# Scale half of the conditioning first, four gate tiles multiplied before the shift is known

## What is computed

```python
mod = c @ w_ada + b_ada                      # c: 1 prompt row and 8 sample rows; w_ada (2048, 6144)
shift, scale, gate = jnp.split(mod, 3, axis=-1)
h = _rms(x, g_norm) * (1 + scale[:, None, :]) + shift[:, None, :]
z = h @ w_in      # parts q, k, v, qi, ki, wi, ga, u, gb, ma, mb
...               # indexer top-k, gathered attention, pooling mixer: attn, pool
a  = (attn * jax.nn.silu(ga)) @ w_a_proj
bb = (pool * jax.nn.silu(gb)) @ w_b_proj
m = jax.nn.sigmoid(ma) * a + jax.nn.sigmoid(mb) * bb
y = x + gate[:, None, :] * (m @ w_out)       # then a final RMSNorm
```

## Time and profile before

| | |
|---|---|
| median of three timed executions | 1974.14 us |
| profiled execution: device time / span | 1972.96 / 1971.1 us |
| busy in the span: PE / DVE / ACT / POOL | 1907.3 / 983.0 / 535.1 / 906.5 us |
| DMA | 257.91 MB, mean 131 GB/s |
| granted clock, mean of the span | 0.985 |

### The profile page before, as it was taken

How to read it: one execution, slowest core, us unless ns; L and a number is a source line. 1 busy time by engine, 2 the same in 40 slices (tenths; PEclk the granted TensorE clock), 3 DMA queues, 4 the chain that set the end, 5 groups by cost and what they waited for, 6 DMA issues and landing times.

```text
span 1971.1 us, 34676 instructions
## 1 busy us (share of the span) xinstructions
PE 1907.3 (97%) x14418; PEld 1767.4 (90%) x14418; DVE 983.0 (50%) x1485; ACT 535.1 (27%) x730; POOL 906.5 (46%) x760
## 2 busy tenths in 40 slices
PE   5789999999999999999999999999999999999997
PEld 2369998989999999999999999999999999887775
DVE  4168885677787778753346444445011411142223
ACT  4122333434333333332211222212222311122223
POOL 0234555545554545444444444445566443344442
PEclk9789999999999999999999999999999999999999
DMA  9963334543233232324332333335475565544333
GB/s 351 360 209 88 105 106 127 151 145 81 79 86 96 75 96 69 96 81 127 87 87 66 96 88 80 88 96 139 139 233 174 175 211 152 174 144 136 107 106 129
DMA packets 325028, 257.91 MB, mean 131 GB/s; under 512 B 8603, under 2 KB 275031, under 8 KB 323623
## 3 DMA queue, kind: packets, MB, share of 16 engines
q1 hardware_dynamic: 311759, 227.03, 39.2%
q0 software_dynamic: 5120, 16.77, 2.6%
q10 hardware_dynamic: 8064, 12.87, 2.2%
HBM read 245.63 MB, written 11.48 MB: 130 GB/s over the span
## 4 chain that ended last, share of the span: by engine, by line
PE 90%; DMA 3%; DVE 2%; SPq 2%; ACT 1%; POOL 1%; issue 1%; DVEq 0%; ACTq 0%
PE acc L1487 68%; PE ps L1941 9%; DMA ring<-in_w_ada 2%; PE ps L1725 1%; PE ps L1601 1%; PE ps L1741 1%; PE ps L1713 1%; PE acc L1500 1%; PE ps L1487 1%; PE acc L1932 1%; PE ps L1871 1%; SPq L334 1%; PE ps L1788 1%; POOL wlo L481 1%; DMA kib<-in_cache_kidx,pgr 1%; PE ps L1647 1%
## 5 line engine op out<-in xcount | busy, mean ns | idle before, releaser
L481 POOL TENSOR_TENSOR wlo<-raw,whi 128x512 fp32r<-128x512 f32 (+1 forms) x612 | 785.4, 1314 | 842.8 <-ACT whi L607 842.8
L1487 PE MATMUL acc<-act_hi,whi 128*128 128x260 f32 (+1 forms) x3520 | 751.2, 289 | 1.7 <-DVE stok L1117 0.9
L1487 PE MATMUL acc<-act_hi,wlo 128*128 128x260 f32 (+1 forms) x3520 | 740.3, 287 | 0.0
L1487 PE MATMUL acc<-act_lo,whi 128*128 128x260 f32 (+1 forms) x3520 | 739.2, 286 | 0.0
L1487 PEld LDWEIGHTS acc<-act_hi,whi 128*128 128x128 f32 x3520 | 551.7, 189 | 18.5 <-issue 13.6
L1487 PEld LDWEIGHTS acc<-act_lo,whi 128*128 128x128 f32 x3520 | 549.9, 188 | 0.7
L1487 PEld LDWEIGHTS acc<-act_hi,wlo 128*128 128x128 f32 x3520 | 549.9, 188 | 0.0
L607 ACT CAST whi<-raw 128x2048 fp32r<-128x2048 f32 (+1 forms) x153 | 279.3, 1825 | 964.4 <-PE acc L1487 764.4
L1941 PE MATMUL ps<-whi,act_hi 128*128 128x512 f32 x256 | 102.1, 399 | 0.0
L1941 PE MATMUL ps<-whi,act_lo 128*128 128x512 f32 x256 | 101.1, 395 | 0.0
L1941 PE MATMUL ps<-wlo,act_hi 128*128 128x512 f32 x256 | 101.0, 394 | 0.0
(11 more groups left out here) (310 smaller groups left out, 2099.1 us busy)
## 6 DMA issues: line engine op xcount, KB each, us to landing
raw<-in_w_in SPq DMA_DIRECT2D x105, 1024.0 KB, 5.9
ring<-in_w_ada SPq DMA_DIRECT2D x32, 1024.0 KB, 9.4
raw<-in_w_a_proj SPq DMA_DIRECT2D x16, 1024.0 KB, 7.9
gate_unit<-in_w_ada SPq DMA_DIRECT2D x16, 1024.0 KB, 7.0
raw<-in_w_out SPq DMA_DIRECT2D x16, 1024.0 KB, 5.1
raw<-in_w_b_proj SPq DMA_DIRECT2D x16, 512.0 KB, 4.6
x_tok<-in_x_prompt SPq DMA_DIRECT2D x4, 1024.0 KB, 16.4
att_dram<-silu_ga ACTq DMA_DIRECT2D x16, 256.0 KB, 2.6
```

The source lines that it names most:

```text
L481: return nc.gpsimd.tensor_tensor(wlo[p][:, a:b], raw[p][:, a:b], whi[p][:, a:b].bitcast(F32), ALU.subtract)
L1487: last = mm(o, w, x[:, k, s], start=(k == 0 and n == 0), stop=(k == kt - 1 and n == 2))
```

## The change

The scale chunks come first, then the shift chunks. With the scale alone VectorE makes `H` without the shift (`scale`), and it and ScalarE split this. TensorE multiplies it by the first four `mb` tiles (`EARLY`): two in quarters between the units 4 to 19, the third with units 20 to 23 and the fourth with units 24 to 29 inside. ScalarE writes the four results to DRAM (`early_out`). Then the shift is added (`shift`), and the split is made again. The index key and the first index query, which were made in parts between the units, are made whole behind the last unit.

The shift's share of those four tiles (shift @ `w_in`, nine columns) is made in the pooled stage: SP loads the four tiles' weights again in four 1 MB units, TensorE makes four `corr_product` and one `corr_columns`, and the four results come back from DRAM to `big2`; ScalarE takes their tanh with the prompt's column as the bias. The pooled stage then has 12 pairs, and four `w_b` tiles without an `mb` tile. The 16 late rounds are spread over 12 pairs: two in each of the pairs 1 to 4.

SP now loads the sample rows and the four token tiles first, then units 0 to 3 (in the places of `whi` and `wlo`) and two `mb` tiles; units from 4 on go round the four buffers in the tokens' place. The first DMAs of ScalarE's queue (conditioning rows and identity) have a semaphore of their own, and the rest of the tables is waited for later.

```diff
-ADA_CHUNKS = [4, 0, 5, 1, 6, 2, 7, 3]
+ADA_CHUNKS = [4, 5, 6, 7, 0, 1, 2, 3]
...
-LATE, LATE_RING = 10, 4
...
+LATE, LATE_RING = 4, 4
...
+RING_AT = [u + 2 if u < LATE else RING + (u - LATE) % LATE_RING for u in range(ADA_UNITS)]
...
+EARLY = 4
+Q_A, Q_B, Q_C, Q_D, Q_E, Q_E1, Q_F1, Q_F2, Q_G, Q_END = 2, 11, 15, 31, 39, 51, 53, 61, 69, 77
+
+N_A, N_B, N_C, N_D, N_E, N_E1, N_F1, N_F2, N_G = 2, 11, 13, 29, 37, 49, 51, 59, 67
...
+    def early_at(e):
+
+        return ((e + 1) // 2, 1 - e % 2)
...
+        def load_early(e, first=False):
+            load(*early_at(e), cols(w_in, C_MB + P * e), first=first)
+
+        sp.dma_start(xs[:], t["x_sample"].rearrange("b s d -> (b s) d")).then_inc(S("xs_landed"), 16)
+        for i in range(4):
+            sp.dma_start(x_tok[:, i, :], t["x_prompt"][0, i * P:(i + 1) * P, :]).then_inc(S(f"x_landed{i}"), 16)
+        sp.dma_start(pgi[:], t["page_table"].rearrange("(o b) n -> o b n", o=1).broadcast_to([P, NB, PAGES])
+                     ).then_inc(S("pages_landed"), 16)
         for u in range(ADA_UNITS):
             if u == LATE:
+                load_early(0, first=True)
+                load_early(1, first=True)
                 sp.wait_ge(S("xT_done"), 4)
...
+            if u == 14:
+                load_early(2)
+            if u == 18:
+                load_early(3)
+            if u == 28:
+                load(Q_A, 1, cols(w_in, C_KI))
...
+        load(Q_A + 1, 0, cols(w_in, C_QI))
+        sp.wait_ge(S("ring_done"), ADA_UNITS)
+        sp.dma_start(cosT[:], t["k_cos"]).then_inc(S("consts_landed"), 16)
+        sp.dma_start(sinT[:], t["k_sin"]).then_inc(S("consts_landed"), 16)
         load(Q_A + 1, 1, cols(w_in, C_QI + P))
...
+
+        for j in range(1, KT - EARLY):
+            load(Q_E + j, 0, cols(w_in, C_MB + P * (EARLY + j)))
+            load(Q_E + j, 1, cols(w_b, P * (EARLY + j)))
+            if j <= 4:
+                if j == 1:
+                    sp.wait_ge(S("early_step"), 1)
+                else:
+                    sp.wait_ge(S("corr_mm"), j - 1)
+                sp.dma_start(corr_unit[:].rearrange("p (k n) -> p k n", n=512), quarter(w_in, j - 1, C_MB)
+                             ).then_inc(S("weights_landed"), 16)
+            if j == 5:
+                sp.wait_ge(S("mix_mm"), 8)
+                sp.wait_ge(S("u_tok_ready"), 8)
+                sp.wait_ge(S("early_stored"), 16 * EARLY)
+                sp.dma_start(big2[:, 0:EARLY, :], early_dram.rearrange("e p n -> p e n")
+                             ).then_inc(S("early_landed"), 16)
+        for n in range(EARLY):
+            load(Q_E1 + n // 2, n % 2, cols(w_b, P * n))
...
-        with pool.Fori(Q_E, Q_F1) as q:
+        with pool.Fori(Q_E, Q_E1) as q:
...
+            lo(q, 1, n=1024)
+        with pool.Fori(Q_E1, Q_F1) as q:
+            lo(q, 0, n=1024)
             lo(q, 1, n=1024)
...
+                         (ident[:], t["k_ident"])):
+            act.dma_start(dst, src).then_inc(S("consts_landed"), 16)
...
-        act.wait_ge(S("tables_landed"), 11 * 16)
...
+        def act_high(g, shifted=False):
+            if shifted and g < 3:
+                act.wait_ge(S("act_spent"), g + 1)
+            elif shifted:
+                act.wait_ge(unit_done[0], 2)
...
+        def early_out(e):
+            p, n = 1 - e % 2, e // 2
+            act.wait_ge(unit_done[p], n + 1)
+            if n:
+                act.wait_ge(S("early_stored"), 32)
+            nc.scalar.copy(halves(xstage[p][:]), accv[p]).then_inc(acc_free[p], 1)
+            act.wait_ge(acc_free[p], n + 1)
+            act.dma_start(early_dram[e], xstage[p][:]).then_inc(S("early_stored"), 16)
...
+        squares(2)
+        x_columns(0)
+        squares(3)
+        x_columns(1)
+        x_columns(2)
+        x_columns(3)
...
+        hi(*early_at(0), first=True)
...
-        act.wait_ge(S("ring_done"), RING_LAST[3] + 1)
-        hi(Q_A, 1, first=True)
-        mod_rows(3)
-        act_high(1)
+        hi(*early_at(1), first=True)
+        for c in range(1, 4):
+            mod_rows(c)
+            act_high(c)
+        early_out(0)
+        hi(*early_at(2))
+        early_out(1)
         mod_rows(4)
+        hi(*early_at(3), done=1)
         mod_rows(5)
-        act_high(2)
+        early_out(2)
+        hi(Q_A, 1)
+        act_high(0, shifted=True)
+        act_high(1, shifted=True)
         mod_rows(6)
+        act_high(2, shifted=True)
         mod_rows(7)
...
-        merge_b(KT - 1, n=2048)
-        act.wait_ge(acc_free[1], N_E + KT)
+        act.wait_ge(S("early_step"), 3)
+        for e in range(EARLY):
+            nc.scalar.activation(big2[:, e, 0:SEQ], big2[:, e, 0:SEQ], ACT.Tanh, scale=0.5, bias=early_bias[:, e:e + 1])
...
+        def scale(g):
             ks = slice(4 * g, 4 * g + 4)
...
+            dve.wait_ge(S("mod_T"), g + 1)
+            step(v.tensor_tensor(mA[:, ks, :], modT[g][:, 1], per_tok(bT[:, 16:32], g), ALU.add))
+            step(v.scalar_tensor_tensor(mA[:, ks, :], mA[:, ks, :], 1.0, per_tok(gT, g), ALU.add, ALU.mult))
             step(v.tensor_tensor(H[:, ks, SEQ:TOK], H[:, ks, SEQ:TOK], mA[:, ks, 1:9], ALU.mult))
+            for k in range(4 * g, 4 * g + 4):
+                v.tensor_scalar(H[:, k, 0:SEQ], H[:, k, 0:SEQ], mA[:, k, 0:1], None, ALU.mult
+                                ).then_inc(S("H_ready"), 1)
+                if k > 4 * g:
+                    act_low(k - 1)
+            act_low(4 * g + 3)
+
+        def shift(g):
+            ks = slice(4 * g, 4 * g + 4)
+            dve.wait_ge(S("mod_T"), 4 + g + 1)
+            step(v.tensor_tensor(mB[:, ks, :], modT[g][:, 0], per_tok(bT[:, 0:16], g), ALU.add))
             step(v.tensor_tensor(H[:, ks, SEQ:TOK], H[:, ks, SEQ:TOK], mB[:, ks, 1:9], ALU.add))
             for k in range(4 * g, 4 * g + 4):
-                v.tensor_scalar(H[:, k, 0:SEQ], H[:, k, 0:SEQ], mA[:, k, 0:1], mB[:, k, 0:1], ALU.mult, ALU.add
+                v.tensor_scalar(H[:, k, 0:SEQ], H[:, k, 0:SEQ], mB[:, k, 0:1], None, ALU.add
...
+        def shifted_low(g):
             for k in range(4 * g, 4 * g + 4):
-                act_low(k)
...
+        for g in range(4):
+            scale(g)
...
+        shift(0)
+        shift(1)
+        shifted_low(0)
+        shifted_low(1)
+        shift(2)
+        shifted_low(2)
+        shift(3)
+        shifted_low(3)
...
+        dve.wait_ge(S("consts_landed"), 5 * 16)
+        rope(Q_A, 1, N_A, kiT[:], S("ki_ready"), 1)
...
+        last.then_inc(acc_free[0], 1)
...
+        for j in range(1, 5):
+            chain.enter(j, j, 8)
+            late_round(2 * j - 1, merged=j)
+            late_round(2 * j)
+            chain.leave(1)
...
+        merge_b(KT - EARLY)
+        dve.wait_ge(S("early_ready"), 1)
+        for n in range(EARLY):
+            p = n % 2
+            dve.wait_ge(unit_done[p], Q_E1 + n // 2 + 1)
+            v.scalar_tensor_tensor(halves(big2[:, n, :]), halves(big2[:, n, :]), 1.0, accv[p], ALU.add, ALU.mult
+                                   ).then_inc(acc_free[p], 1)
...
+        def early_quarter(e, g):
+
+            tile(*early_at(e), 0, parts=S("act_lo_ready"), free=False, ks=range(4 * g, 4 * g + 4))
...
-        pe.wait_ge(S("tables_landed"), 11 * 16)
+        pe.wait_ge(S("consts_landed"), 3 * 16)
...
-        tr(ps[:, 1, 16:64], rows_b[:], ident[0:48, 0:48])
-        tr(ps[:, 1, 64:88], rows_gs[:], ident[0:24, 0:24]).then_inc(S("rows_T"), 1)
-        pe.wait_ge(S("cT_ready"), 1)
+        tr(ps[:, 1, 0:16], rows_cp[:], ident[0:16, 0:16]).then_inc(S("front_T"), 1)
+        pe.wait_ge(S("front_set"), 2)
...
-            if u % 4 == 1 and u >= 5:
+            if u % 4 == 0 and u:
...
+
+        sample_columns_T()
+        for u in range(4):
+            token_columns(u)
+            if u == 1:
+                table_columns()
+            unit(u)
+        pe.wait_ge(S("xT_act"), 4)
+        pe.wait_ge(S("xT_dve"), 4)
+        quarters_after = {5: [(0, 0)], 7: [(1, 0)], 10: [(0, 1)], 11: [(1, 1)], 14: [(0, 2)], 15: [(1, 2)],
+                          18: [(0, 3), (1, 3)]}
+        for u in range(4, 20):
+            unit(u)
+            for e, g in quarters_after.get(u, ()):
+                early_quarter(e, g)
+
+        def units_in_second(part):
+            unit(20 + part)
+
+        def units_in_third(part):
+            if part < 3:
+                unit(24 + 2 * part)
+                unit(25 + 2 * part)
+
+        tile(*early_at(2), 1, hi_first=True, between=units_in_second)
+        tile(*early_at(3), 1, between=units_in_third, spent=S("act_spent"))
+        unit(30)
+        unit(31)
+        index_key(0)
         mod_columns(7)
-        index_key(10, 12)
+        for g in range(1, 4):
+            index_key(g)
         for r in range(4):
             wi_product(r)
-        index_key(12, 16)
-        first_query(3)
+        tile(Q_A + 1, 0, N_A, hi_first=True, query=True)
...
+        def corr_product(i):
+            if i == 0:
+                pe.wait_ge(S("early_step"), 1)
```

(46 more changed lines are left out.)

252 lines of the change are left out of this document (111 added, 141 removed).

## The result

The changed kernel takes 1957.38 us (median of four, 1956.76 to 1960.7) beside 1973.8 us for the kernel before: a ratio of 0.9918, 95% interval 0.9907 to 0.993. It is faster by 16 us, the forecast was 17.4. The profiled execution is the slowest of the four (1960.7 us of device time): its span is 12.2 us shorter than that of the kernel before, where the medians differ by 16.4. A second trace of the same kernel stands among the experiments.

The account below looks back on a forecast made before the run. TensorE was taken as the bound, busy nearly everywhere, with room only in the front. Front +24.7, matmuls behind the keys -1.6 and pooled stage -40.5 sum to -17.4 us: 1957 us, range 1948 to 1972.

Parts of the forecast that it names:

- Pooled stage, -40.5: Pooled stage: four tiles leave (-46.1 us), correction units and column step add 5.0, a late first unit 0.6.
- Rival (3): Pooled stage: VectorE becomes the bound in pairs 1 to 4, taking 17.6 us, about 1974 us; chance 0.06.
- Tokens at 31.2: Front: ScalarE starts at 6.7 us, so at the old pace the token transposes are done at 31.2 us.
- SP's wait at nothing: Front: SP's wait for the tokens before unit 4 costs nothing, as queued transfers last to 32.5 us, 1.3 to spare.
- Unit 4 at 35.2: Front: unit 4 lands at 35.2 us, after nine units' transfers, two tiles and 3.4 us lost at the start.
- Unit 18 done at 88.1: Front: TensorE's work and waits give 80.1 us, transfers 81.5; with 8 us of clock loss, 88.1.
- The clock loss: Front up to unit 18: TensorE's reduced clock costs 8 us, taken as half, between nothing and 15.7.
- its sign: Front: before unit 18's matmuls, near 88 us, TensorE waits for VectorE or GpSimd rather than for the ring.
- the rival (2): Units 19 to 31: the transfer queue runs dry 2 us per unit, losing 12.4 us, 1969 us; chance 0.11.
- From unit 18 to the keys, 79.9: Unit 18 to the key transposes: TensorE's work sums to 79.9 us at full clock, putting the transposes at 168.0.
- The 4.1 us wait and the 1.6: Key transposes: the 4.1 us wait for VectorE goes; ten matmuls after it run at full clock, saving 1.6 us.
- Rival (1): Front: TensorE stays at 1.2 GHz for units 4 to 18 and the last quarters, +34.1 us, 1991 us; chance 0.12.

Follow-up runs that it names:

- the thin tiles: Changed kernel with most products of the four early gate tiles left out (33.8 us of matmuls), their loads, casts and low parts kept: 1952.9 us, ratio 0.9884.
- the later second load: Changed kernel with the second early tile's load issued behind unit 5 rather than ahead of unit 4: 1957.9 us, ratio 0.9908.
- the reordered front: Changed kernel with the second early tile's load behind unit 5, third and fourth behind units 18 and 21, second tile's first quarter behind unit 9: 1952.3 us.
- three single edits of the front: Changed kernel with, one at a time, 28 useless products before unit 4, second early tile's cast first, or its load later: 1958.8, 1959.5, 1957.9 us.
- the changed kernel with filler: Changed kernel plus 28 useless identity products between units 3 and 4, nothing left out: 1958.8 us, ratio 0.9914.
- the reordered front with filler: The reordered front plus 18 useless identity products in the wait between units 3 and 4, nothing left out: 1952.6 us, ratio 0.9890.
- the last version: The reordered front with the second early tile's load behind unit 9, its cast and quarters later, plus 18 useless products before unit 4: 1952.5 us, ratio 0.9889.

## Why the prediction held, and where it was right for another reason

**Pooled stage, -40.5: right, 40.56 measured.** The four tiles are 46.12 (46.1). The columns cost 5.56: 1.17 a unit rather than 1.0 and 0.87 for the step; the 0.6 for a late first unit came to nothing, as the first pair is no longer than the others (18.45). VectorE, the tanh and the way through DRAM cost nothing that shows: without the columns the stage is shorter by the four tiles to 0.02 us. Rival (3) is out, with 3.35 us to spare.

**Tokens at 31.2, and SP's wait at nothing: right**, 30.65 and a share of 1.10. The forecast reckoned the old pace (24.5 us) from an earlier first square (6.7). In fact the square starts at 8.00 and the tokens take 22.7 us more, and the pace hangs on the order of the loads: with the order undone the square starts as early, at 7.99, but the tokens are done only at 38.3. So the earlier start by itself is worth 2.8 of the 10.4 us, and 6 to 8 us at the keys hang on the order, which my later theory had at next to nothing.

**Unit 4 at 35.2: 3.2 us too early.** The sum left out a dip: from 12.5 to 15 us the share is 0.54, which costs some 1.2 us at 1.05. But in the second trace the share there is 0.85, and unit 4 starts no earlier (38.5). What the 3.2 us are made of isn't settled.

**Unit 18 done at 88.1: 91.1 and 89.4 measured, by other means.** The clock loss, 8 us in the forecast, is about 6 (busy time by one minus the clock: 5 us from 40 to 90, the rest on either side); the waits for GpSimd and VectorE, 8 us in the forecast without unit 5's, are 4.6 in the first trace. But the step that failed is the choice of the limit: the forecast let TensorE's work set unit 18 and found the transfers done at 81.5, and its sign, waits for VectorE or GpSimd rather than for the ring ahead of unit 18, didn't come. TensorE waits for the ring there, 2.93 and 3.03 us, and with 11.5 us less work, in the thin tiles, unit 18 starts at the second trace's time (87.8 and 87.9).

The transfers were later than reckoned. Unit 4 came 3.2 us late. From 50 to 60 us the queue ran dry, some 4 us by its share (0.63 against 1.05): all four ring places were full, and SP waited up to 7.6 us for one, while TensorE made the first quarter at half clock, stood at the second tile's low part and made that tile's quarter, partly at half clock. That is the rival (2)'s mechanism, a queue run dry, but ahead of unit 18 and not behind it. It isn't the whole: with a full queue there, the later second load still waits for the ring and starts unit 18 at 86.2.

In the reordered front unit 18 is done at 82.1. That this is near the 81.5 of the forecast's transfers is chance: with two tiles fewer ahead of unit 18, the same sum gives 74.1. TensorE doesn't wait for unit 18 there; its own work, half clock up to 47 us and some short waits set the time, for which the forecast had 80.1 at full clock.

**From unit 18 to the keys, 79.9: 82.2 and 82.1.** The index key is mis-sized: with the column step inside it takes 14.1 us (138.13 to 152.27) and not 12.5, as the last group's split isn't wholly hidden by two quarters; the rest is mainly half clock behind unit 18 (0.87 from 90 to 100). Behind unit 19 no wait for DMA is over 0.2 us, as forecast; but the thin tiles show that TensorE is the limit there only narrowly.

**The 4.1 us wait and the 1.6: right.** The keys start without a wait, and the ten matmuls behind them that took 3.41 us take 1.87:

```profile
174.25 0.42 PE L1599 MATMUL acc<-act_hi,whi 128*128 128x392 f32 x1
...
176.12 0.34 PE L1599 MATMUL acc<-act_lo,whi 128*128 128x392 f32 x1
```

The whole stretch from the keys to the pooled stage's start can't show it: it takes 927.2 and 928.5 us in the two traces against 928.95 before, and scatters by more than that (last section).

**Sum.** Front 28.2 against 23.1 in the first trace: 5.1 too little. The forecast's 1957.0 stands beside 1957.4 by luck: the traced execution lies 3.3 us above its median, while the forecast put its own 1.2 below, and that hides most of the error. By the ratios the change gives 16.2 and 15.6 us (two sets of executions), not 17.4. The order of the first loads is worth some 5.9 of them; whether that order alone would have helped the kernel before, with no tile moved, no run tried.

**Rival (1), the clock.** The first trace has half clock in parts of 30 to 60 us and 0.88 over 40 to 90, and 1.00 from 140 to 175: partly borne out, not for the whole stretch that it needed. With fewer products and longer waits the clock is lower: from 80 to 140 us it is 0.80 in the thin tiles, which wait 15.1 us for the ring, against 0.97 in the changed kernel, which is idle 3.1 us in all. The Trainium skill, "TensorE: Matmul & The Clock Gate", section "Loop structure matters more than you think", says that a loop with a long wait for DMA between matmuls lets TensorE go cold; these rows agree.

## What to carry to other kernels

Work moved into a stretch that waits for transfers can be nearly free: leaving 33.8 us of the moved products out again gave back only 5 to 7. But count what the moved work displaces: here the index key and the first query, which had filled some of that stretch, had to go behind it, and the front grew by 28.2 us for 46.1 us of moved tiles. What costs besides is a wait that holds up the release of buffers, as the queue can then run dry; so put the product that may wait behind the units that free the ring, and loads that aren't yet needed behind those that are. Try edits against neighbouring limits together: none of three single edits of the front could be told from none by its time, a set gave 6.5 us. Which members of the set are needed stays open, as two of them weren't tried alone.

## What the runs showed of the hardware

In the three kernels with filler the clock was 1.00 from 30 to 40 us, while the useless products ran, but it fell afterwards: to 0.83 from 50 to 60 us in the changed kernel with filler, to 0.53 there in the reordered front with filler, which was busy 9.12 us of these 10, and in the last version to 0.66 already from 40 to 50. And what stands far behind the edits moves by as much as they: from the keys to the pooled stage the traces of kernels with the same code there take 923.8 (the last version) to 930.5 us (second load later). One part of it lies near 900 us: TensorE pauses there for 3.1 us in each of the traces looked at, and behind the pause the clock falls in some executions and not in others. The first matmul behind the pause and a window of the changed kernel, and then of the one with the filler:

```profile
905.82 0.77 PE L1850 MATMUL ps<-prob_hi,v_part 128*128 128x512 f32 x1 [3.07 <-issue]
```

```profile
900.00:1000.00 100.00, 96.66 (x754) 94.86 (x753) 34.64 (x67) 19.91 (x19) 39.20 (x28) 0.97 0.38 106
```

```profile
904.01 0.47 PE L1852 MATMUL ps<-prob_hi,v_part 128*128 128x512 f32 x1 [3.07 <-issue]
```

```profile
900.00:1000.00 100.00, 94.90 (x760) 93.06 (x759) 37.23 (x69) 21.11 (x20) 41.60 (x30) 1.00 0.36 100
```

A mean clock that is lower by 0.03 over 97 busy us is 3 us, as much as most single edits of the front bring.
